# Delta heads: the keys' roots ahead of the queries', their mean on VectorE, and the scaled keys for w ahead of the third weight split

## The reference

```python
def _l2norm(x):
    return x * lax.rsqrt(jnp.sum(x * x, axis=-1, keepdims=True) + EPS)

qd, kd, vd = _split(jax.nn.silu(conv), [D_QK, D_QK, D_W])
qd = _l2norm(_heads(qd, D_HEADS)) * D_DK ** -0.5
kd = _l2norm(_heads(kd, D_HEADS))
...
kb = kc * bc                                   # keys by beta
a_mat = jnp.where(strict, kb @ kc^T * gam, 0.0)
rhs = [vc * bc, kb * exp(G)]
u0, w = triangular_solve(a_mat + eye, rhs)
attn = qc @ kc^T * gam
kg = kc * exp(G[-1] - G)
u = u0 - w @ S;  o = (qc * exp(G)) @ S + attn @ u;  S = exp(G[-1]) * S + kg^T @ u
```

## Time and profile before

| | |
|---|---|
| timed runs, median (lowest to highest) | 1605.67 us (1605.19 to 1609.41) |
| profiled execution, own time | 1610.02 us |
| profiled execution, span of its instructions | 1608.2 us |
| TensorE busy | 1514.3 us (94% of the span) |
| VectorE busy | 979.7 us (61%) |
| ScalarE busy | 628.3 us (39%) |
| GpSimd busy | 180.8 us (11%) |
| mean granted TensorE clock | 0.973 |

### The profile page before, as it was taken

How to read it: one execution, slowest core, us unless ns; L and a number is a source line. 1 busy time by engine, 2 the same in 40 slices (tenths; PEclk the granted TensorE clock), 3 DMA queues, 4 the chain that set the end, 5 groups by cost and what they waited for, 6 DMA issues and landing times. The chain is left out here.

```text
span 1608.2 us, 30737 instructions
## 1 busy us (share of the span) xinstructions
PE 1514.3 (94%) x11056; PEld 1415.6 (88%) x11056; DVE 979.7 (61%) x2122; ACT 628.3 (39%) x1491; POOL 180.8 (11%) x384
## 2 busy tenths in 40 slices
PE   6999999999999999799799999899999999977998
PEld 2689999998999999799699999899999998966998
DVE  2666565665867767733576664577677667754622
ACT  2523232322232332423564442355555455543521
POOL 1000000000000000001000001023222312312000
PEclk9999999999999999899799999999999999988899
DMA  9343433441552433233441502311211121020223
GB/s 335 107 115 95 110 95 108 102 126 39 118 154 80 116 103 99 63 97 101 119 83 50 130 21 63 96 43 46 71 44 55 44 59 41 6 74 4 89 89 118
DMA packets 195260, 141.01 MB, mean 88 GB/s; under 512 B 18332, under 2 KB 178584, under 8 KB 194916
## 3 DMA queue, kind: packets, MB, share of 16 engines
q1 hardware_dynamic: 177772, 130.22, 28.6%
q10 hardware_dynamic: 17400, 9.60, 2.2%
HBM read 128.65 MB, written 11.15 MB: 87 GB/s over the span
## 5 line engine op out<-in xcount | busy, mean ns | idle before, releaser
L182 PE MATMUL bank<-hT,w_high 128*128 128x288 f32 x1152 | 361.4, 314 | 6.0 <-ACT retention_qkT_raw L1272 2.1
L183 PE MATMUL bank<-hT,w_low 128*128 128x288 f32 x1152 | 342.7, 298 | 0.0
L184 PE MATMUL bank<-hT,w_high 128*128 128x288 f32 x1152 | 342.7, 297 | 0.0
L182 PEld LDWEIGHTS bank<-hT,w_high 128*128 128x128 f32 x1152 | 220.5, 191 | 7.6 <-DVE w_low L974 2.9
L183 PEld LDWEIGHTS bank<-hT,w_low 128*128 128x128 f32 x1152 | 220.3, 191 | 0.0
L184 PEld LDWEIGHTS bank<-hT,w_high 128*128 128x128 f32 x1152 | 219.6, 191 | 0.0
L182 PE MATMUL bank<-output_w_split,gT_high 128*128 128x256 f32 x512 | 143.4, 280 | 0.0
L184 PE MATMUL bank<-output_w_split,gT_high 128*128 128x256 f32 x512 | 143.2, 280 | 0.0
L183 PE MATMUL bank<-output_w_split,gT_low 128*128 128x256 f32 x512 | 142.7, 279 | 0.0
L183 PEld LDWEIGHTS bank<-output_w_split,gT_low 128*128 128x128 f32 x512 | 96.6, 189 | 0.0
L182 PEld LDWEIGHTS bank<-output_w_split,gT_high 128*128 128x128 f32 x512 | 96.3, 188 | 0.1
(11 more groups left out here) (491 smaller groups left out, 3589.2 us busy)
## 6 DMA issues: line engine op xcount, KB each, us to landing
x<-in_w_in_even SPq DMA_DIRECT2D x72, 512.0 KB, 5.3
x<-in_w_in_odd SPq DMA_DIRECT2D x56, 512.0 KB, 4.5
x<-in_w_ada SPq DMA_DIRECT2D x32, 256.0 KB, 4.7
front_w_ada<-in_w_ada SPq DMA_DIRECT2D x6, 1024.0 KB, 15.6
output_w_raw<-in_w_out_even SPq DMA_DIRECT2D x12, 512.0 KB, 3.4
output_w_raw<-in_w_out_odd SPq DMA_DIRECT2D x12, 512.0 KB, 3.5
gdn_E<-G_rows SPq DMA_DIRECT2D x8, 576.0 KB, 5.1
gT<-in_w_ada SPq DMA_DIRECT2D x16, 256.0 KB, 3.4
```

The lines of the kernel that those rows point to most:

```text
L182: pe.matmul(out, w[0], x[1], start=first, stop=False)
L183: pe.matmul(out, w[1], x[0], start=False, stop=False)
L184: return pe.matmul(out, w[0], x[0], start=False, stop=last)
```

## The change

The sums' mean goes from GpSimd to VectorE, right behind the reduction. GpSimd's one root over ten columns becomes two over five, the keys' first. The keys' factor and the scaling of the keys wait for the first only; the queries' factor is computed after the keys are scaled. The two factor products and `kbe` move from behind `attnT` to ahead of `low(dve, ahead, 2)`. A wait for the constant -0.5 is added once, ahead of the loop.

```diff
-                 ... "ms_ready": 1, "rn_ready": 1, "scale_a": 1, "scale_b": 1,
+                 ... "ms_ready": 1, "rn_ready": 2, "scale_a": 2, "scale_b": 1,
...
             dve.tensor_reduce(ss[:], sqs, AX.X, ALU.add).then_inc(s["ss_ready"].sem, 1)
+            dve.wait_ge(*s["ss_ready"].done(h, 0))
+            dve.tensor_scalar(ms[:], ss[:], 0.25, EPS, ALU.mult, ALU.add).then_inc(s["ms_ready"].sem, 1)
...
             dve.wait_ge(*s["kg_scaled"].before(h, 0))
-            dve.tensor_scalar(sc[:, 0, :], rn[:, :, 1], 0.5, None, ALU.mult)
-            dve.tensor_scalar(sc[:, 1, :], rn[:, :, 0], 0.5 * P ** -0.5, None, ALU.mult).then_inc(s["scale_a"].sem, 1)
+            dve.tensor_scalar(sc[:, 0, :], rn[:, :, 1], 0.5, None, ALU.mult).then_inc(s["scale_a"].sem, 1)
             dve.wait_ge(*s["scale_a"].done(h, 0))
...
             dve.tensor_tensor(kn[:], tk[:, :, 1, :], spread(sc[:, 0, :]), ALU.mult)
+            dve.wait_ge(*s["rn_ready"].done(h, 1))
+            dve.tensor_scalar(sc[:, 1, :], rn[:, :, 0], 0.5 * P ** -0.5, None, ALU.mult).then_inc(s["scale_a"].sem, 1)
+            dve.wait_ge(*s["scale_a"].done(h, 1))
             dve.tensor_tensor(qn[:], tk[:, :, 0, :], spread(sc[:, 1, :]), ALU.mult).then_inc(s["kq_norm"].sem, 1)
...
+            dve.tensor_tensor(sc[:, 2, :], sc[:, 0, :], gcol(1), ALU.mult)
+            dve.tensor_tensor(sc[:, 3, :], sc[:, 0, :], gcol(3), ALU.mult).then_inc(s["scale_b"].sem, 1)
+            dve.wait_ge(*s["scale_b"].done(h, 0))
+            dve.tensor_tensor(kbe[:], tk[:, :, 1, :], spread(sc[:, 2, :]), ALU.mult).then_inc(s["kv_scaled"].sem, 1)
             low(dve, ahead, 2)
...
-            dve.tensor_tensor(sc[:, 2, :], sc[:, 0, :], gcol(1), ALU.mult)
-            ...
-            dve.tensor_tensor(kbe[:], tk[:, :, 1, :], spread(sc[:, 2, :]), ALU.mult).then_inc(s["kv_scaled"].sem, 1)
...
-            pool.wait_ge(*s["ss_ready"].done(h, 0))
+            pool.wait_ge(*s["ms_ready"].done(h, 0))
             pool.sem_inc(M.passed, 1)
-            pool.tensor_scalar(ms[:], ss[:], 0.25, EPS, ALU.mult, ALU.add).then_inc(s["ms_ready"].sem, 1)
-            pool.wait_ge(*s["ms_ready"].done(h, 0))
-            pool.tensor_tensor(rn[:], ms[:], mh[:], ALU.pow).then_inc(s["rn_ready"].sem, 1)
+            for i in (1, 0):
+                pool.tensor_tensor(rn[:, :, i], ms[:, :, i], mh[:, :, i], ALU.pow).then_inc(s["rn_ready"].sem, 1)
```

More of the change, by code:

```diff
@@ L1692, in gdn_heads @@
                  "z_ready": 1,
-                 "tok_psum": T, "tok_copied": T, "tok_squared": 1, "ss_ready": 1, "ms_ready": 1, "rn_ready": 1, "scale_a": 1, "scale_b": 1,
+                 "tok_psum": T, "tok_copied": T, "tok_squared": 1, "ss_ready": 1, "ms_ready": 1, "rn_ready": 2, "scale_a": 2, "scale_b": 1,
                  "kq_norm": 1, "kq_psum": 1, "kq_copied": 1, "kk_psum": 1, "A_ready": 1, "attn_ready": 1, "level_ready": NL,
@@ L1706, in gdn_heads @@
         first = FirstLoads(ph, M, IN, "output1")
-        cleared = sig("cleared")
+        cleared, half_set = sig("cleared"), sig("half_set")
         cacheT_psum, cacheT_copied, cache_stored = sig("cache_psum", 2), sig("cache_copied", 2), sig("cache_stored", 32)
@@ L2162, in dve_turn @@
             dve.tensor_tensor(atT[:, 0:SEQ], PS[3][:, :], E[:, 0, 0:SEQ], ALU.mult).then_inc(s["attn_ready"].sem, 1)
-            dve.tensor_tensor(sc[:, 2, :], sc[:, 0, :], gcol(1), ALU.mult)
-            dve.tensor_tensor(sc[:, 3, :], sc[:, 0, :], gcol(3), ALU.mult).then_inc(s["scale_b"].sem, 1)
-            dve.wait_ge(*s["scale_b"].done(h, 0))
-            dve.tensor_tensor(kbe[:], tk[:, :, 1, :], spread(sc[:, 2, :]), ALU.mult).then_inc(s["kv_scaled"].sem, 1)
             for n in range(NL):
@@ L2278, in _ @@
                 ph.clear_left()
-                pool.memset(mh[:], -0.5)
+                pool.memset(mh[:], -0.5).then_inc(half_set.sem, 1)
+                pool.wait_ge(*half_set.done(0, 0))
                 with pool.Fori(0, H) as h:
```

## The result

The changed kernel takes 1593.3 us, the median of four runs (1592.19 to 1595.19); the kernel before took 1607.49 in the four runs of the same comparison (1605.19 to 1609.41). The ratio is 0.9914 with an interval of 0.9893 to 0.9934, so 13.8 us less by the ratio. The forecast was 1596.1, 9.6 us less, range 1593.0 to 1603.0; it was laid from 1605.67, the median of three runs of the kernel before.

What follows compares the result with a forecast made beforehand. TensorE, busy 94% of the span, was taken as the bound, so only its waits counted. Gains of 4.0 us (mean and roots) and 5.6 (moved factors and kbe) took 1605.67 to 1596.1 us, range 1593.0 to 1603.0.

Steps and rivals of the forecast that it cites:

- rival 3: Roots of five columns cost what ten do, 1.97 us each; queries 1.1 us late a head; 1608.9 us; chance 0.07.
- rival 1: At the scaling of the keys, the queries' root keeps VectorE out until it ends; 1600.8 to 1603.1 us; chance 0.18.
- rival 2: Factor product L2164 costs 1.38 us wherever it stands; L2152 0.63 late in seven heads; 1600.5 us; chance 0.13.
- Rival 4: The keys' root isn't blocked by VectorE's L2116; 12.3 us gained, 1593.4 us; chance 0.10.
- the sum: Gains at TensorE's waits over all heads: 4.0 us from the first part, 5.6 from the second, together 9.6 us less.
- Part one: Mean on VectorE and root in two steps: queries ready 0.5 us earlier for L1904, 4.0 us in eight heads.
- Part two: Factor products and kbe ahead of the split: 0.89 us at L1949 in six heads, 0.3 in head seven, 5.6 together.

Runs made afterwards that it cites:

- the control: The kernel before run again without a change, against the kernel before: 1610.0 against 1607.45, ratio 1.0004; the rest of its span 1158.61 us.
- the run with the waiting masks: Kernel before, with GpSimd's second group of five masks (level 1) waiting until kbe is done: 1605.51 against 1607.45, ratio 0.9983.
- The joined masks: Kernel before, with GpSimd waiting for the end of its first five masks before the next five: 1601.9 against 1608.14, ratio 0.996.

## Why the prediction was right, step by step

**The mechanism held at every step.** Against the reduction's start: the mean ends at +1.69, forecast +1.69. The keys' root ends 1.04 us after the end of VectorE's instruction for z, as forecast to the hundredth; it stands at +3.43 against +3.40. The root of five columns costs 1.165 to 1.175 (forecast 1.18), so rival 3 is out. The scaling of the keys beside the second root takes 0.824 to 0.826 in eight of eight heads, so rival 1 is out. By the rule that the prediction cited from the Trainium skill (SBUF — State Buffer, section SBUF: two separate sides) whoever starts first keeps the port for the whole instruction. By rival 1, which works this out for this kernel, the scaling of the keys would have ended near +5.30, after the second root; it started at +3.67 and ended at +4.49, before the root did (+4.56). The trace disagrees with that rule for a root of five columns too, and agrees for z against the root (0.37 us in the run with the mean alone). The small product is 0.151 to 0.164 in its new place, and L2160 still idles 0.59 ahead of itself: rival 2 is out. Rival 4 (no block by z) is out by the 1.56 us of the keys' root.

**The sizes were a little low.** The stage gave 11.8 us where the sum said 9.6:

- Part one: L1904 came 0.59 earlier, not 0.5. The queries were scaled by +5.63 where the steps said +5.75; the second root ended 0.05 sooner, and between factor and scaling there were 0.03 us, not the 0.12 taken from the kernel before.
- Part two: L1943 to L1949 shrank by 0.91, forecast 0.89.
- Not in the sum at all: L1904 to L1917 lost 0.10 (I said unchanged) and L1949 to L1957 lost 0.12. The first shows in the wait for L2169, 0.17 where it was 0.26. It arises between TensorE's second group of L1910 and VectorE's `AT`, which starts 1.37 us after that group's start before and 1.26 after. All runs with the split roots have the shorter time, and no row names its cause. TensorE before, then after:

```profile
1105.56 1.23 PE L1910 MATMUL bank<-gdn_qT,gdn_kT 128*128 128x128 f32 x10
```
```profile
1098.65 1.23 PE L1910 MATMUL bank<-gdn_qT,gdn_kT 128*128 128x128 f32 x10
```

- The second stands in the rows: the ten products of L1949 took 1.28 us behind their wait, and 1.17 without one. In heads one to six the step fell by 1.70 to 1.81, where 1.39 was forecast; over six heads that is 2.1 of the missing 2.2.
- Head seven gave 0.93 (0.8 forecast) and the last 0.45 (0.5).

Adding only the terms that I could name was the cautious side of the sum; the small ones all pointed the same way.

**The measured time lies inside the range with some luck.** It is 0.3 us above the lower edge. The range was laid from 1605.67; the kernel before had 1607.49 in the comparison, and laid from there it would have begun at 1594.8. The change again had 1596.88, but against 1609.87 for the kernel before on that chip. The gain of the stage, 11.8, lies nearer to rival 4's 12.3 than to the 9.6 of the sum, and 1593.3 is nearly rival 4's 1593.4. So the time alone would speak for rival 4; it is the keys' root of 1.56 us that rules it out.

**What the timed runs show beyond the stage** is 13.8 - 11.8 = 2.0 us, inside the interval of the ratio (10.6 to 17.2 us). The 5.5 us between the rests of the two first profiles are not shown to be an effect of the change: the control moved by 2.5, the change's second profile has 1153.12, and kernels with and without it mix between 1150.6 and 1158.6.

**The weak reason behind a right step.** I argued that L2164's price comes from the masks beside it, and it does. But I took this as a plain sharing of the port, which would have made the run with the waiting masks a gain of 4.5 to 6.5 us. It gave 1.05. As far as the runs show, the price is set by where in the chain of masks the instruction falls. The change works because it puts a covered instruction (the copy) where an uncovered one stood.

## What to carry to other kernels

A slow step on a helper engine that feeds two consumers can be worth cutting in two if its price falls with its size (here one root of 1.96 us became two of 1.17): the second half lies beside the first consumer, and the first consumer can be let go at once, which gave the further 4.0 us here. When a small instruction of VectorE shows ten times its price, look at what GpSimd runs beside it; move it where GpSimd is idle, or let GpSimd wait for its own instruction of few rows before the next (5.15 us in the stage of the kernel before, nothing once the held instruction was covered). Before moving something out of such a slot, ask which instruction slides in, and whether it is covered.

## What the runs showed of the hardware

- GpSimd's root over 128 rows: 0.552 us for one column, 1.165 to 1.175 for five, 1.964 for ten, a straight line of about 0.39 + 0.158 a column.
- Behind a mask of 64 rows, followed by further masks without a wait, VectorE was kept out for about four masks: the factor product took 1.38 us instead of 0.15, L1834 took 2.12 instead of 0.82. With the short mask third, L2160 took 2.40 instead of 0.43, some six masks. With a wait in between it was one mask, 0.39 instead of 0.15. It hit products and copies alike.
- The other way round, a mask beside L1834 took 1.00 us instead of 0.41, and L1834 its usual 0.82.
- Why is not shown. The Trainium skill (GPSIMD Engine Reference, section 2.1 Instruction dispatch) says that GpSimd's cores each serve 16 partitions and start the next instruction as soon as their own share is done. If so, half of the cores would run ahead behind 64 rows, and some core would be reading at nearly all times until a wait joins them again. The joined masks agree with that (0.39 instead of 1.38), and so does the place at which the hold began with the other order of masks. Its end does not fit as well: there L2160 was done at 1111.36, while the chain's last mask ran from 1111.24 to 1111.64, with no wait before it. No run here looked at single cores.
